# Score products of 64-wide heads issued in pairs, and one weight chunk split inside the double norm

## The chip, the cores and the metric

The kernel runs on one core of a Trainium2 chip. The metric is the device time of one execution in microseconds (us). The core's engines are TensorE (PE, with its weight loads shown as PEld), VectorE (DVE), ScalarE (ACT), GpSimd (POOL) and SyncE (SP), which only issues transfers here. Each runs its own list of instructions in order and waits for the others on semaphores.

## The reference, cut to what matters

Three transformer blocks follow each other on 256 tokens of width 1024. What is computed at the places of the change are attentions whose heads are 64 wide, and the norm between block 1 and block 2:

```python
# block 1, even layer: sliding window, 8 query heads of 64, 2 key/value heads, a sink for each head
logits = jnp.einsum('bkgnqd,bknsd->bkgnqs', qb, kb).astype(jnp.float32) * (DH ** -0.5) + bias
probs = jax.nn.softmax(jnp.concatenate([logits, sink], axis=-1), axis=-1)[..., :-1]
...
# block 2, layer 0 (the "mixer"): differential attention, 8 score heads of 64, beside a short convolution
z = hn @ a_w_in[j]
...
attn = diff_attention(q, k, v, lam, lambda_init, a_subln[j])
...
# block 3: latent attention (8 heads, 96 wide), then sparse attention (8 heads, 64 wide), 256 + 16 keys
s = jnp.einsum('bqhd,bqkhd->bhqk', qb, k_sel, preferred_element_type=jnp.float32) * scale
```

Block 1 ends in `rmsnorm(h, final_gain)` and block 2 begins with `rms_norm(h, ln_mix[0])`, so two norms stand in a row there: the double norm.

## The kernel before

**Weights.** All weight matrices come as one stream of chunks of 1 MB (128 rows, 2048 columns) into a ring of three buffers, in two halves each. ScalarE casts a half to `high` (L252, `split_high`), VectorE subtracts it from the original to get `low` (L261, `split_low`), and SyncE loads the chunk three later into the slot when the subtraction is done (L227). A cast also waits until TensorE has used the chunk three before (`used`). TensorE multiplies with both parts (`times`, L276 to L278: high by high, high by low, low by high). A chunk of an input projection is 48 such products, 24 for each tile of 128 tokens (`chunk_pe`).

**Projections.** Chunk m of a projection goes to PSUM bank m % 2, and ScalarE evicts it (`evac_act`, L1278), scaled by the norm's factor. From the third chunk on TensorE waits for the eviction of the chunk two before (`evac`).

**The double norm.** The first chunk of the mixer is multiplied with h as it is, while the norm's factor is still being worked out; the factor is applied at the eviction, which waits for `scaled`. In `deferred_act` ScalarE squares h, then `roots_act` squares the gained h (L526), when VectorE has made it, and takes two roots (L518). In `scale_twice_dve` VectorE gains h (L579), makes the mean (L562, L564), refines the first root (`newton`, L363 to L371), works out the second mean (L585 to L589), refines the second root, signals `scaled` (L592) and scales h (L595). Behind that, in the programs of the mixer (`mixer_act`, `mixer_dve`), both engines split the third chunk, whose number is `c0 + 2`; the first two were split earlier.

**Attention.** All five attentions are run by `Steps`. Step s on TensorE (`step_pe`) has three parts: the scores of head s (L1051, two products, one for each tile of queries), the product of head s − 2 with the values (L1068), and the transposes of head s − 1 (L1079, in block 3 also L1083). VectorE masks (L1126, signals `masked_l`) and takes maxima (L1130); ScalarE makes the exponentials (L1097, and L1099 where there is a sink; `soft`) and copies the transposed rows (L1111, L1113; `spread`); VectorE scales the output (L1155). Heads take two score banks in turn, so the scores of head s wait for the mask of head s − 2. Other work stands between the steps: in the sliding-window attention and in the sparse attention six products of 512 columns of the output projection (`half_pe`), in the mixer 24 products of a chunk. A 64-wide head lies on rows 0 to 63 of its operands if its number is even, on 64 to 127 if it is odd. The layout of the heads of the latent attention (96 wide) and of block 1's odd layer (128 wide) has no such pairs.

Of the kernel before, what the change touches and what calls it, by code (L numbers as in the profile page):

```python
# [17 lines left out]
NT = SEQ // P  # L18
# [16 lines left out]
TWO = (P, P)  # L35
# [497 lines left out]
def deferred_act(A, k, gain, sem, first, last, twice=False, start=False):  # L533

    turn_act(A, k, TWO, 4, k.xT[0], gain, at=4)
    if start:
        split_high(A, k, k.main, A.chunk)
    A.e.wait_ge(sem, A.passed.get(sem.num, 0) + first)
    A.step(square_act(A, k, 0))
    preload(A, k, ACT.Sqrt)  # L540
    turn_act(A, k, TWO, 4, k.xT[0][:, 4:8, :], gain, at=6, k0=4)
    if start:
        A.e.wait_ge(k.s["x_last"], 16)
    else:
        A.e.wait_ge(*A.next(sem, last))
    A.join()
    A.tell(square_act(A, k, 1), k.s["squared"])
    roots_act(A, k, twice)
    if start:
        split_high(A, k, k.main, A.chunk + 1)  # L550
# [22 lines left out]

def scale_twice_dve(V, k):

# [4 lines left out]
    V.tell(ins, k.s["gained"])  # L580
    var, tmp = mean_dve(V, k)
    newton(V, k, r1, var, tmp)
    V.join()
# [428 lines left out]
class Steps:  # L1012


    def __init__(self, heads, keys, q, kk, values, blocks, scale, bias, out, dv, score, prob, outs, meta=None,
                 sink=None, gate=None):
        self.heads, self.keys, self.q, self.kk, self.values, self.blocks = heads, keys, q, kk, values, blocks
# [26 lines left out]
def step_pe(T, k, a, s):  # L1044

    ident = k.const("ident")
    if s < a.heads:
        if s >= len(a.score):
            T.e.wait_ge(*T.next(k.s["masked_l"]))
        for t in range(NT):  # L1050
            ins = T.e.matmul(a.scores(k, s)[:, a.at[t]:a.at[t] + a.keys[t]], a.q(s, t), a.kk(s)[:, 0:a.keys[t]],  # L1051
                             start=True, stop=True)
        T.tell(ins, k.s["scored"])
    h = s - 2
# [189 lines left out]

def chunk_pe(T, k, m, tiles, after=None, within=None):

# [4 lines left out]
    if m >= 2:  # L1251
        T.e.wait_ge(*T.next(k.s["evac"]))
    for t, rows in enumerate(tiles):
        out = k.ps[0:rows, m % 2, t * CW:(t + 1) * CW] if t < NT else k.ps[0:rows, 2, 0:CW]
        if t == NT and m:
# [12 lines left out]

def evac_act(A, k, dst, m, func=None, at=None, r=None):

    A.e.wait_ge(k.main.used, A.chunk + 1)
    got = k.ps[:, m % 2, :].rearrange("p (t w) -> p t w", t=NT)
    at = m * CW if at is None else at
# [101 lines left out]
class Even:  # L1375
# [31 lines left out]
    def swa(self, k):  # L1407
# [6 lines left out]
        def rows(n):  # L1414
# [6 lines left out]
            (6, 7), ((3, 0), (4, 0)), ((3, 384), (4, 384)), sink=lambda n: sinks[:, head(n):head(n) + 1],  # L1421
            gate=lambda n: pr[:, :, 1536 + head(n) * 64:1536 + (head(n) + 1) * 64])

# [462 lines left out]
def block1_dve(V, k):  # L1886
# [11 lines left out]
    odd_dve(V, k)  # L1898
    scale_twice_dve(V, k)

# [94 lines left out]
class Mixer:  # L1995
# [11 lines left out]
    def steps(self, k):  # L2007
        def rows(h):
# [5 lines left out]
            lambda h: k.const("causal"), lambda h: self.both[:, :, h // 2, h % 2, :], P,  # L2014
            (3, 4), ((5, 0), (6, 0)), ((2, 0), (7, 0)))

# [22 lines left out]
def mixer_pe(T, k):  # L2039
# [3 lines left out]
    for n in range(1, 4):  # L2043
        chunk_pe(T, k, n, TWO)
    jobs = Jobs(T, k, m.jobs, MIXER_BANKS)
# [34 lines left out]
def mixer_act(A, k):  # L2080
# [4 lines left out]
    for n in range(4):  # L2085
        split_high_next(A, k, c0 + n + 2)
        if n == 0:
            scaled(A, k)
        evac_act(A, k, m.pr, n, r=r)
    preload(A, k, ACT.Exp)  # L2090
# [26 lines left out]
def mixer_dve(V, k):  # L2117
# [6 lines left out]
    V.next(k.s["evac"], N_IN2)  # L2124
    for n in range(4):
        split_low_next(V, k, c0 + n + 2)
    V.e.wait_ge(k.s["evac"], evac + 4)
# [986 lines left out]
class Third:  # L3114
# [41 lines left out]
    def dsa(self, k):  # L3156
# [5 lines left out]
        def rows(h):  # L3162
# [4 lines left out]
            lambda h: k.mix[:, :, 512 + h * 64:512 + (h + 1) * 64], 64,  # L3167
            (3, 4), ((5, 0), (6, 0)), ((5, 384), (6, 384)), 7)

# [776 lines left out]
```

## Time and profile before

| | |
|---|---|
| median of 3 runs | 1884.21 us (1884.13 to 1884.23) |
| the profiled execution | 1883.01 us, of which 1880.8 us from the first to the last instruction (the span) |
| TensorE busy | 1827.9 us, 97% of the span |
| VectorE busy | 1402.7 us, 75% |
| ScalarE busy | 1205.2 us, 64% |
| TensorE clock granted, mean | 0.992 of full |

Times in a timeline count from the span's start. A record of TensorE's begins when the product begins; its end is modelled and overlaps the next, so the distance from one start to the next is what a product takes. An fp32 product is two records. Idle time is shown in square brackets with the engine and the line that ended it. In the rows a clock of 1.00 is 2.4 GHz and 0.50 is 1.2 GHz. Block 1's sliding window lies at 95 to 127 us, the double norm at 250 to 261, the mixer's attention at 286 to 327, the sparse attention at 1630 to 1667.

### The profile page before, as it was taken

Reading aid. Unit: us, or ns where it says so; the run is one execution under the profiler, and the core shown is the slowest. Engines: PE = TensorE matmul, PEld = TensorE weight load, DVE = VectorE, ACT = ScalarE, POOL = GpSimd, SP = SyncE. Lnnn points to the kernel's source line nnn. Section 1 sums busy time; section 2 is a strip of 40 time slices with the busy share of each in tenths; the row PEclk is TensorE's granted clock in tenths of the full one; section 3 lists DMA queues with packets and bytes.
Section 4 is the critical chain, followed back from the end, with each engine's and each line's share of the span. In section 5 each row is a group of like instructions: output and inputs, shape, how many; then the busy total and the mean of one; then the engine's idle time right before and its main releaser. Section 6 shows DMA issues by size and latency. Waiting matters only on the chain.

```text
span 1880.8 us, 31987 instructions
## 1 busy us (share of the span) xinstructions
PE 1827.9 (97%) x11013; PEld 1590.8 (85%) x11013; DVE 1402.7 (75%) x2039; ACT 1205.2 (64%) x1897; POOL 71.8 (4%) x109
## 2 busy tenths in 40 slices
PE   8989999999999999999999999999999999999998
PEld 7969889899989878888888888888887888889997
DVE  5575765855566669998989998989999777666555
ACT  6556555544456557877878787878778666454444
POOL 2000000000000020000000000000000033200000
PEclk9999999999999999999999999999999999999999
DMA  8526344465555459999999999999999443136552
GB/s 297 196 92 221 116 135 126 150 201 178 190 168 193 156 162 386 366 374 367 370 363 367 366 373 365 361 361 358 366 362 351 151 136 101 57 107 196 189 189 91
DMA packets 129571, 454.05 MB, mean 241 GB/s; under 512 B 15182, under 2 KB 20206, under 8 KB 129216
## 3 DMA queue, kind: packets, MB, share of 16 engines
q1 hardware_dynamic: 119920, 435.74, 65.6%
q10 hardware_dynamic: 8544, 13.30, 2.2%
q0 software_dynamic: 1008, 3.67, 0.5%
q8 instruction: 65, 1.06, 0.2%
q14 instruction: 34, 0.28, 0.0%
HBM read 450.53 MB, written 5.27 MB: 242 GB/s over the span
## 4 chain that ended last, share of the span: by engine, by line
PE 91%; DVE 5%; ACT 3%; issue 1%; DMA 0%; ACTq 0%; DVEq 0%
PE ps L276 27%; PE ps L277 27%; PE ps L278 27%; PE ps L1068 2%; PE ps L1051 1%; DVE low L261 1%; PE ps L2736 1%; DVE xT_low L342 1%; PE ps L2802 1%; PE ps L410 1%; PE ps L973 1%; PE ps L1079 1%; ACT xT_high L330 1%; ACT high L252 0%; PE ps L2718 0%
## 5 line engine op out<-in xcount | busy, mean ns | idle before, releaser
L261 DVE TENSOR_TENSOR low<-ring,high 128x1024 fp32r<-128x1024 f32 x828 | 980.3, 1223 | 211.9 <-ACT high L252 209.4
L252 ACT CAST high<-ring 128x1024 fp32r<-128x1024 f32 x828 | 834.5, 1050 | 189.1 <-PE ps L278 154.8
L276 PE MATMUL ps<-high,xT_high 128*128 128x256 f32 (+2 forms) x1848 | 639.5, 346 | 20.5 <-DVE xT_low L342 7.1
L277 PE MATMUL ps<-low,xT_high 128*128 128x256 f32 (+2 forms) x1848 | 621.7, 336 | 0.0
L278 PE MATMUL ps<-high,xT_low 128*128 128x256 f32 (+2 forms) x1848 | 619.1, 335 | 0.0
L276 PEld LDWEIGHTS ps<-high,xT_high 128*128 128x128 f32 (+1 forms) x1848 | 347.3, 188 | 63.2 <-issue 14.4
L278 PEld LDWEIGHTS ps<-high,xT_low 128*128 128x128 f32 (+1 forms) x1848 | 347.0, 188 | 40.3
L277 PEld LDWEIGHTS ps<-low,xT_high 128*128 128x128 f32 (+1 forms) x1848 | 348.1, 188 | 33.1
L276 PE MATMUL ps<-high,smallT_high 128*128 128x512 f32 (+2 forms) x582 | 225.0, 387 | 0.7 <-DVE smallT_low L342 0.5
L277 PE MATMUL ps<-low,smallT_high 128*128 128x512 f32 (+2 forms) x582 | 225.3, 387 | 0.0
L278 PE MATMUL ps<-high,smallT_low 128*128 128x512 f32 (+2 forms) x582 | 224.3, 385 | 0.0
L276 PE MATMUL ps<-xT_high,high 128*128 128x256 f32 x704 | 198.4, 282 | 0.6 <-DVE xT_low L342 0.6
L277 PE MATMUL ps<-xT_low,high 128*128 128x256 f32 x704 | 198.6, 282 | 0.0
L278 PE MATMUL ps<-xT_high,low 128*128 128x256 f32 x704 | 197.5, 281 | 0.0
L276 PEld LDWEIGHTS ps<-xT_high,high 128*128 128x128 f32 x704 | 132.2, 188 | 1.8 <-issue 0.9
L278 PEld LDWEIGHTS ps<-xT_high,low 128*128 128x128 f32 x704 | 133.1, 189 | 0.0
L277 PEld LDWEIGHTS ps<-xT_low,high 128*128 128x128 f32 x704 | 132.4, 188 | 0.8
L276 PEld LDWEIGHTS ps<-high,smallT_high 128*128 128x128 f32 (+1 forms) x582 | 109.5, 188 | 24.8 <-DVE smallT_low L342 0.8
L278 PEld LDWEIGHTS ps<-high,smallT_low 128*128 128x128 f32 (+1 forms) x582 | 109.2, 188 | 24.2
L277 PEld LDWEIGHTS ps<-low,smallT_high 128*128 128x128 f32 (+1 forms) x582 | 109.2, 188 | 22.6
L823 ACT ACTIVATE work<-work 128x256 f32<-128x256 f32 x44 | 18.4, 418 | 104.3 <-DVE work L860 104.3
L1278 ACT ACTIVATE proj<-ps,small 128x256 f32<-128x256 f32 x82 | 34.3, 470 | 56.0 <-PE ps L278 56.0
(357 smaller groups left out, 1428.1 us busy)
## 6 DMA issues: line engine op xcount, KB each, us to landing
ring<-in_stream SPq DMA_DIRECT2D x828, 512.0 KB, 5.1
bias_rows<-bias_line ACTq DMA_DIRECT2D x2, 1536.0 KB, 12.8
wide<-in_wide_rows ACTq DMA_DIRECT2D x5, 512.0 KB, 5.4
work<-bias_rows ACTq DMA_DIRECT2D x2, 1024.0 KB, 9.4
h<-in_x SPq DMA_DIRECT2D x2, 512.0 KB, 4.8
work<-bias_rows ACTq DMA_DIRECT2D x2, 512.0 KB, 6.5
token_rows<-mix ACTq DMA_DIRECT2D x1, 1024.0 KB, 4.6
consts<-in_consts ACTq DMA_DIRECT2D x1, 870.0 KB
```

Source lines behind the costliest of these rows:

```text
L252: A.e.copy(k.high[:, slot, cols], k.ring[:, slot, cols]).then_inc(flow.high_made, 1)
L261: V.e.tensor_tensor(k.low[:, slot, cols], k.ring[:, slot, cols], k.high[:, slot, cols].bitcast(F32), ALU.subtract).then_inc(flow.split, 1)
L276: T.e.matmul(out, x[0], w[0], start=start, stop=False, **more)
L277: T.e.matmul(out, x[0], w[1], start=False, stop=False, **more)
L278: return T.e.matmul(out, x[1], w[0], start=False, stop=stop, **more)
L330: ins = A.e.activation(high[:, kt, 0:width], k.ps[:, at + b % 4, n * width:(n + 1) * width], ACT.Copy, scale=g)
L342: ins = V.e.scalar_tensor_tensor(low[:, kt, 0:width], k.ps[:, at + b % 4, n * width:(n + 1) * width], g, high[:, kt, 0:width].bitcast(F32) ...
L410: ins = T.e.transpose(k.ps[:, 4 + b, (n * NT + t) * P:(n * NT + t + 1) * P], k.h[:, t, kt * P:(kt + 1) * P], k.const("ident"))
L973: ins = T.e.transpose(k.ps[0:width, self.banks[n % nb], at:at + P], src, k.const("ident"))
L1051: ins = T.e.matmul(a.scores(k, s)[:, a.at[t]:a.at[t] + a.keys[t]], a.q(s, t), a.kk(s)[:, 0:a.keys[t]], start=True, stop=True)
L1068: ins = T.e.matmul(out, left, a.values(h, b), start=(b == 0), stop=(b == last))
L1278: ins = A.e.activation(dst[:, t, at:at + CW], got[:, t, :], func or ACT.Copy, scale=r[:, t:t + 1])
```

## The change

Three things are done.

1. `Steps` gets a flag `paired`, set for the sliding-window attention, the mixer and the sparse attention. With it an even step issues the scores of heads s and s + 1, tile by tile in turn, and waits for two masks; an odd step issues none.
2. The split of the mixer's third chunk moves into the double norm: ScalarE's two casts behind its last square of h, VectorE's two subtractions behind the first mean. The mixer's own loops then split each chunk one place earlier.
3. The third chunk goes to PSUM bank 2, and TensorE does not wait for an eviction before it.

```diff
@@ deferred_act
     A.tell(square_act(A, k, 1), k.s["squared"])
+    if twice:
+        split_high_next(A, k, A.chunk + 2)
     roots_act(A, k, twice)
@@ scale_twice_dve (block 1 passes V.chunk + 2, block 2 nothing)
     var, tmp = mean_dve(V, k)
+    if ahead is not None:
+        split_low_next(V, k, ahead)
     newton(V, k, r1, var, tmp)
@@ step_pe
-    if s < a.heads:
+    if s < a.heads and not (a.paired and s % 2):
+        group = (s, s + 1) if a.paired else (s,)
         if s >= len(a.score):
-            T.e.wait_ge(*T.next(k.s["masked_l"]))
+            T.e.wait_ge(*T.next(k.s["masked_l"], len(group)))
         for t in range(NT):
-            ins = T.e.matmul(a.scores(k, s)[:, a.at[t]:a.at[t] + a.keys[t]], a.q(s, t), a.kk(s)[:, 0:a.keys[t]],
-                             start=True, stop=True)
-        T.tell(ins, k.s["scored"])
+            for h in group:
+                ins = T.e.matmul(a.scores(k, h)[:, a.at[t]:a.at[t] + a.keys[t]], a.q(h, t), a.kk(h)[:, 0:a.keys[t]],
+                                 start=True, stop=True)
+                if t == NT - 1:
+                    T.tell(ins, k.s["scored"])
@@ chunk_pe
     if m >= 2:
-        T.e.wait_ge(*T.next(k.s["evac"]))
+        evac = T.next(k.s["evac"])
+        if bank is None:
+            T.e.wait_ge(*evac)
@@ mixer_pe
     for n in range(1, 4):
-        chunk_pe(T, k, n, TWO)
+        chunk_pe(T, k, n, TWO, bank=2 if n == 2 else None)
@@ mixer_act
     for n in range(4):
-        split_high_next(A, k, c0 + n + 2)
+        if n < 3:
+            split_high_next(A, k, c0 + n + 3)
         if n == 0:
             scaled(A, k)
-        evac_act(A, k, m.pr, n, r=r)
+        evac_act(A, k, m.pr, n, r=r, bank=2 if n == 2 else None)
@@ mixer_dve
-    for n in range(4):
-        split_low_next(V, k, c0 + n + 2)
+    for n in range(3):
+        split_low_next(V, k, c0 + n + 3)
```

How the order of instructions moves, at three places. Line numbers of the changed kernel are 2 to 11 higher than those of the same lines before (L1058 is the score product, L1076 the product with the values, L1087 the transposes, L1288 the eviction).

ScalarE through the double norm, before (L511 squares h, L526 squares the gained h, L518 is a root, L252 a cast, L1278 the eviction of the first chunk):

```order
L511 ACTIVATE work,small<-h 128x512 [waits act_steps,added]
L511 ACTIVATE work,small<-h 128x512
L526 ACTIVATE mix,small<-work 128x1024 [waits gained]
L526 ACTIVATE mix,small<-work 128x1024
L518 ACTIVATE small<-small 128x2 [waits var_made] x2
L252 CAST high<-ring 128x1024 [waits chunk_used,chunk_landed1_0]
L252 CAST high<-ring 128x1024 [waits chunk_landed1_1]
L1278 ACTIVATE proj<-ps,small 128x256 [waits chunk_used,scaled]
L1278 ACTIVATE proj<-ps,small 128x256
L252 CAST high<-ring 128x1024 [waits chunk_used,chunk_landed2_0]
```

and now:

```order
L511 ACTIVATE work,small<-h 128x512 [waits act_steps,added]
L511 ACTIVATE work,small<-h 128x512
L252 CAST high<-ring 128x1024 [waits chunk_used,chunk_landed1_0]
L252 CAST high<-ring 128x1024 [waits chunk_landed1_1]
L526 ACTIVATE mix,small<-work 128x1024 [waits gained]
L526 ACTIVATE mix,small<-work 128x1024
L518 ACTIVATE small<-small 128x2 [waits var_made] x2
L252 CAST high<-ring 128x1024 [waits chunk_used,chunk_landed2_0]
L252 CAST high<-ring 128x1024 [waits chunk_landed2_1]
L1288 ACTIVATE proj<-ps,small 128x256 [waits chunk_used,scaled]
```

The two casts of slot 1, the third chunk's, stand ahead of the squares of the gained h; behind the roots the casts of slot 2 follow at once.

TensorE in the sliding-window attention, before: from the transposes of step 2 to the product with the values of step 3.

```order
L1079 MATMUL ps<-consts,logit 128x128 [waits soft]
L1079 MATMUL ps<-consts,logit 128x128 x2
L276 MATMUL ps<-high,xT_high 128x512
L277 MATMUL ps<-low,xT_high 128x512
L278 MATMUL ps<-high,xT_low 128x512
L276 MATMUL ps<-high,xT_high 128x512
L277 MATMUL ps<-low,xT_high 128x512
L278 MATMUL ps<-high,xT_low 128x512
L1051 MATMUL ps<-proj 128x128 [waits masked_l]
L1051 MATMUL ps<-proj 128x256
L1068 MATMUL ps<-proj,probT 128x64 [waits spread]
L1068 MATMUL ps<-proj,probT 128x64 x2
```

Now, the scores of step 2 with what stands around them,

```order
L277 MATMUL ps<-low,xT_high 128x512
L278 MATMUL ps<-high,xT_low 128x512
L1058 MATMUL ps<-proj 128x128 [waits masked_l]
L1058 MATMUL ps<-proj 128x128
L1058 MATMUL ps<-proj 128x256 x2
L1076 MATMUL ps<-proj,probT 128x64 [waits spread]
L1076 MATMUL ps<-proj,probT 128x64 x2
```

and from the transposes of step 2 on:

```order
L1087 MATMUL ps<-consts,logit 128x128 [waits soft]
L1087 MATMUL ps<-consts,logit 128x128 x2
L276 MATMUL ps<-high,xT_high 128x512
L277 MATMUL ps<-low,xT_high 128x512
L278 MATMUL ps<-high,xT_low 128x512
L276 MATMUL ps<-high,xT_high 128x512
L277 MATMUL ps<-low,xT_high 128x512
L278 MATMUL ps<-high,xT_low 128x512
L1076 MATMUL ps<-proj,probT 128x64 [waits spread]
L1076 MATMUL ps<-proj,probT 128x64 x2
```

Step 2 has the scores of two heads, and between the products of the output projection and step 3's product with the values none are left.

TensorE where the mixer's third chunk begins, before:

```order
L276 MATMUL ps<-high,xT_high 128x256
L277 MATMUL ps<-low,xT_high 128x256
L278 MATMUL ps<-high,xT_low 128x256
L276 MATMUL ps<-high,xT_high 128x256 [waits evac,chunk_split]
L277 MATMUL ps<-low,xT_high 128x256
L278 MATMUL ps<-high,xT_low 128x256
```

and now:

```order
L276 MATMUL ps<-high,xT_high 128x256
L277 MATMUL ps<-low,xT_high 128x256
L278 MATMUL ps<-high,xT_low 128x256
L276 MATMUL ps<-high,xT_high 128x256 [waits chunk_split]
L277 MATMUL ps<-low,xT_high 128x256
L278 MATMUL ps<-high,xT_low 128x256
```

The wait for an eviction is gone from the first product of the third chunk; the wait for the split stays.

## Rows read from the trace of the kernel before

**Rows 1.** The page's chain that ended last, by engine.

```profile
PE 91%; DVE 5%; ACT 3%; issue 1%; DMA 0%; ACTq 0%; DVEq 0%
```

**Rows 2.** TensorE's timeline, mixer's third chunk: start, length (us), instruction, [idle <-releaser].

```profile
259.59 0.28 PE L278 MATMUL ps<-high,xT_low 128*128 128x256 f32 x1
263.02 0.58 PE L276 MATMUL ps<-high,xT_high 128*128 128x256 f32 x1 [3.15 <-DVE low L261]
```

**Rows 3.** Stretches there: engines' busy us, granted clock, DMA share, GB/s.

```profile
254.30:259.90 5.60, 5.57 (x48) 5.36 (x46) 2.84 (x16) 3.98 (x8) 0.00 (x0) 1.00 0.01 3
259.90:262.90 3.00, 0.00 (x0) 0.00 (x0) 3.00 (x5) 3.00 (x6) 0.00 (x0) 1.00 0.00 0
262.93:266.34 3.41, 3.32 (x15) 3.32 (x16) 3.41 (x5) 2.38 (x4) 0.00 (x0) 0.50 0.92 270
```

**Rows 4.** ScalarE's timeline through the double norm, columns as in rows 2.

```profile
254.08 1.06 ACT L526 ACTIVATE mix<-work 128x1024 f32<-128x1024 f32 x1 [2.04 <-DVE work L579]
...
258.09 1.98 ACT L252 CAST high<-ring 128x1024 fp32r<-128x1024 f32 x2
259.97 0.83 ACT L1278 ACTIVATE proj<-ps,small 128x256 f32<-128x256 f32 x2
```

**Rows 5.** VectorE's timeline through the double norm, columns as in rows 2.

```profile
256.39 0.17 DVE L363 RECIPROCAL small<-small 128x2 f32<-128x2 f32 x1 [2.08 <-ACT small L518]
...
259.29 1.41 DVE L595 TENSOR_SCALAR h<-work,small 128x1024 f32<-128x1024 f32 x2
260.61 6.90 DVE L261 TENSOR_TENSOR low<-ring,high 128x1024 fp32r<-128x1024 f32 x6
```

**Rows 6.** TensorE's timeline, a step of the mixer's attention.

```profile
294.34 0.92 PE L1051 MATMUL ps<-work 64*128 64x128 f32 x4
295.19 0.94 PE L1068 MATMUL ps<-proj,probT 128*128 128x128 f32 x6
```

**Rows 7.** TensorE's timeline, a step of the sparse attention.

```profile
1642.48 0.97 PE L1051 MATMUL ps<-work,proj 64*128 64x144 f32 x4
1643.38 0.43 PE L1068 MATMUL ps<-proj,probM 128*128 128x64 f32 x2
```

**Rows 8.** Stretches of the three attentions, columns as in rows 3.

```profile
102.67:111.99 9.32, 9.32 (x55) 7.04 (x54) 8.52 (x27) 5.29 (x15) 0.00 (x0) 1.00 0.21 63
122.98:126.39 3.41, 1.67 (x14) 1.30 (x13) 2.91 (x14) 1.65 (x6) 0.00 (x0) 1.00 0.01 2
126.39:129.81 3.42, 3.42 (x12) 2.73 (x11) 0.58 (x2) 0.00 (x0) 0.00 (x0) 0.50 0.02 7
287.20:320.00 32.80, 32.80 (x247) 29.53 (x248) 18.85 (x39) 17.91 (x47) 0.00 (x0) 1.00 0.35 114
1639.30:1663.90 24.60, 24.60 (x157) 19.65 (x157) 13.14 (x35) 12.32 (x39) 0.00 (x0) 1.00 0.14 44
```

**Rows 9.** ScalarE's timeline: evictions of the mixer's third and fourth chunk.

```profile
270.47 0.84 ACT L1278 ACTIVATE proj<-ps,small 128x256 f32<-128x256 f32 x2 [5.17 <-PE ps L278]
...
276.13 0.84 ACT L1278 ACTIVATE proj<-ps,small 128x256 f32<-128x256 f32 x2 [2.93 <-PE ps L278]
```

**Rows 10.** TensorE's timeline: index products of heads 0 and 1.

```profile
1558.76 0.98 PE L3202 MATMUL ps<-proj 64*128 64x144 f32 x8
```

**Rows 11.** TensorE's timeline, first transposes of the sparse attention.

```profile
1633.46 0.33 PE L1079 MATMUL ps<-consts,logit 128*128 128x128 f32 x1 [0.56 <-ACT logit L1097]
```

**Rows 12.** TensorE's timeline, waits of the sliding-window attention.

```profile
99.68 0.55 PE L1079 MATMUL ps<-consts,logit 128*128 128x128 f32 x3 [1.06 <-ACT small L1099]
...
124.75 0.55 PE L1079 MATMUL ps<-consts,logit 128*128 128x128 f32 x3 [1.17 <-ACT small L1099]
```

**Rows 13.** VectorE's timeline in the sliding-window attention.

```profile
110.19 0.55 DVE L1126 SCALAR_TENSOR_TENSOR logit<-ps,work 128x384 f32<-128x384 f32 x1
...
113.22 1.23 DVE L261 TENSOR_TENSOR low<-ring,high 128x1024 fp32r<-128x1024 f32 x1 [0.39 <-ACT high L252]
```

**Rows 14.** ScalarE's timeline in the sliding-window attention.

```profile
112.15 1.04 ACT L252 CAST high<-ring 128x1024 fp32r<-128x1024 f32 x1 [2.79 <-PE ps L278]
```

More of the change, by code:

```diff
@@ L571, in scale_h_dve, with scale_twice_dve @@
     return scale_of(k)
-def scale_twice_dve(V, k):
+def scale_twice_dve(V, k, ahead=None):
     gained, r1, r = gained_of(k), first_scale_of(k), scale_of(k)
@@ L1015, in __init__ @@
     def __init__(self, heads, keys, q, kk, values, blocks, scale, bias, out, dv, score, prob, outs, meta=None,
-                 sink=None, gate=None):
+                 sink=None, gate=None, paired=False):
+        self.paired = paired
         self.heads, self.keys, self.q, self.kk, self.values, self.blocks = heads, keys, q, kk, values, blocks
@@ L1239, in load_bias_act, with chunk_pe @@
         A.e.dma_start(bias_of(k)[:, :, t * P:(2 * t + 1) * P], src).then_inc(k.s["bias_loaded"], 16)
-def chunk_pe(T, k, m, tiles, after=None, within=None):
+def chunk_pe(T, k, m, tiles, after=None, within=None, bank=None):
     c = T.chunk
@@ L1251, in chunk_pe @@
     if m >= 2:
-        T.e.wait_ge(*T.next(k.s["evac"]))
+        evac = T.next(k.s["evac"])
+        if bank is None:
+            T.e.wait_ge(*evac)
     for t, rows in enumerate(tiles):
-        out = k.ps[0:rows, m % 2, t * CW:(t + 1) * CW] if t < NT else k.ps[0:rows, 2, 0:CW]
+        out = k.ps[0:rows, m % 2 if bank is None else bank, t * CW:(t + 1) * CW] if t < NT else k.ps[0:rows, 2, 0:CW]
         if t == NT and m:
@@ L1266, in chunk_pe, with evac_act @@
     T.chunk += 1
-def evac_act(A, k, dst, m, func=None, at=None, r=None):
+def evac_act(A, k, dst, m, func=None, at=None, r=None, bank=None):
     A.e.wait_ge(k.main.used, A.chunk + 1)
-    got = k.ps[:, m % 2, :].rearrange("p (t w) -> p t w", t=NT)
+    got = k.ps[:, m % 2 if bank is None else bank, :].rearrange("p (t w) -> p t w", t=NT)
     at = m * CW if at is None else at
@@ L1421, in swa @@
             (6, 7), ((3, 0), (4, 0)), ((3, 384), (4, 384)), sink=lambda n: sinks[:, head(n):head(n) + 1],
-            gate=lambda n: pr[:, :, 1536 + head(n) * 64:1536 + (head(n) + 1) * 64])
+            gate=lambda n: pr[:, :, 1536 + head(n) * 64:1536 + (head(n) + 1) * 64], paired=True)
 EVEN_BANKS, SWA_BANKS = (2, 3), (5, 2)
@@ L1898, in block1_dve @@
     odd_dve(V, k)
-    scale_twice_dve(V, k)
+    scale_twice_dve(V, k, V.chunk + 2)
 def angles_of(k):
@@ L2014, in steps @@
             lambda h: k.const("causal"), lambda h: self.both[:, :, h // 2, h % 2, :], P,
-            (3, 4), ((5, 0), (6, 0)), ((2, 0), (7, 0)))
+            (3, 4), ((5, 0), (6, 0)), ((2, 0), (7, 0)), paired=True)
 MIXER_BANKS = (3, 4, 5, 6)
@@ L3167, in dsa @@
             lambda h: k.mix[:, :, 512 + h * 64:512 + (h + 1) * 64], 64,
-            (3, 4), ((5, 0), (6, 0)), ((5, 384), (6, 384)), 7)
+            (3, 4), ((5, 0), (6, 0)), ((5, 384), (6, 384)), 7, paired=True)
 JOB_BANKS, INDEX_JOB_BANKS, INDEX_BANKS, MLA_BANKS, DSA_BANKS = (3, 4, 5), (0, 6), (6, 7), (3, 4, 5), (3, 4)
```

## The prediction

> **What bounds the kernel now.** I read the chain of waits first: TensorE carries 91% of what ended last [rows 1]. So an edit is worth what it takes off TensorE's own time, or off a wait of TensorE, as long as nothing else is late right behind it. Then I read TensorE's timeline at the two kinds of place that the diff touches.
>
> The first is the start of the second block's mixer. TensorE issues the last product of the second chunk at 259.59 and the first of the third at 263.02, and waited for the `low` half of that chunk [rows 2]. The stretches show what follows: nothing is done from 259.90 to 262.90, and then the granted clock is 0.50 up to 266.34 (1.2 instead of 2.4 GHz) [rows 3]. The third chunk is late because its split stands behind the whole double norm: ScalarE casts it at 258.09, after the second root, and VectorE subtracts at 260.61, after it has scaled h [rows 4, 5].
>
> The second is the score product of a 64-wide head. In the mixer the next operation starts 0.85 us after it (294.34 to 295.19), in the third block's sparse attention 0.90 us (1642.48 to 1643.38) [rows 6, 7]. Whether such time is TensorE's to win depends on the stage. In the mixer VectorE is busy 18.9 of 32.8 us, in the sparse attention 13.1 of 24.6, and TensorE is busy throughout; in the sliding-window attention VectorE is busy 8.5 of 9.3 us, which makes it a second bound there [rows 8].
>
> **The split in the gaps of the norm.** Removed from behind the norm: two casts and two subtractions. They go where both engines are idle. ScalarE stands idle for 2.04 us ahead of the gained h's square at 254.08; two casts take 1.98 us [rows 4]. They fit, and the square that follows is late by 0.05 us at most. Their weights are there: the transfers stand still from 254.30 to 259.90 (DMA share 0.01 [rows 3]), since the ring is full. VectorE is idle for 2.08 us ahead of 256.39, and two of its subtractions take 2.3 (six in 6.90) [rows 5]. Its chain of small operations is thus 0.2 to 0.3 us late, and `scaled` and the scaling of h with it. Nobody on TensorE notices: chunk 3 asks for the eviction of chunk 1. On ScalarE the casts of the fourth chunk now take 258.1 to 260.1, the first eviction 260.1 to 260.9 (it was at 259.97, for it stood behind casts of its own), the casts of the fifth 260.9 to 262.9, the second eviction ends at 263.7. The third chunk, from 259.71, takes 5.66 us (two evictions that wait for TensorE alone start at 270.47 and 276.13 [rows 9]), to 265.4. The slack is 1.7 us. The fourth chunk's `low` half needs VectorE after h, 260.9 to 263.2: slack 2.2 us. The bank 2 that the third chunk takes removes the third wait, that for the eviction of chunk 0, which would else have kept the start at about 260.9.
>
> What this gives: the wait, 263.02 − 259.59 − 0.12 for the product itself = 3.31 us; and the low clock, 263.02 to 266.34 at half rate, 3.32 us for work of 1.66. Together **4.97 us**. What is late next: the ropes wait for the fourth eviction, which moves with TensorE, so the attention starts with the same slack as before. The fewest that I can argue for is 3.3 (the low clock falls somewhere else), the most 5.0.
>
> **The paired products.** The two heads of a pair lie on rows 0 to 63 and 64 to 127 and write to two banks. The trace holds such neighbours already: the index products of two heads, eight records, take 0.98 us, and one head alone, four records of the same shapes, 0.97 [rows 10, 7]. So I take the second head of a pair at nothing, and the saving at the whole place of the odd head. The other end, if the two did not overlap, is a saving near zero. Against pairing speaks a rule of the Trainium skill (TensorE: Matmul & The Clock Gate, "The cost: per-tile semaphore tail"): each increment on a packed product adds some 26 ns, and here each head still signals by itself. By it an estimated 0.3 us of the twelve pairs would be lost; the eight records above carry both heads' signals and show 0.01 us a pair.
>
> The pair needs both masks of the pair before (`masked_l` by 2). The odd one's scores are there a whole step earlier, so VectorE can mask it right after its other work. By stage:
>
> Mixer: four odd heads, 4 × 0.85 = **3.4 us**. Between an even head's scores and its transposes still lie two heads' products with the values, a head's transposes and 24 products of a chunk. TensorE has no wait in these steps now (32.80 of 32.80 us busy [rows 8]), and what goes is 0.85 us between a score and its transposes out of a step of 4.9.
>
> Sparse attention: the first pair wins nothing, since TensorE waits for the first head's exponentials at 1633.46 anyway [rows 11]. The other three give 3 × 0.90 = **2.7 us**; VectorE's 13.1 and ScalarE's 12.3 us of these six steps [rows 8] stay far under the 21.9 that TensorE is left with.
>
> Sliding-window attention: the first pair is lost in the same way (99.68, a wait of 1.06 us [rows 12]). After it VectorE works without a pause: the mask of head 4 at 110.19 comes straight after a subtraction, and names no wait [rows 13]. The one pause until the end is 0.39 us, at 113.22, and it is for a cast that ScalarE began at 112.15, when TensorE had released the chunk [rows 13, 14]. TensorE is there 0.85 us sooner, but VectorE can use 0.39 of it. I take **0.4 us**; the rest comes back as longer waits for the last heads' exponentials, where TensorE already waits 1.17 at 124.75 [rows 12].
>
> **Sum.** 4.97 + 3.4 + 2.7 + 0.4 = 11.5 us. The profiled execution has a span of 1880.8 and a time of 1883.0, the median is 1884.2; the span goes to 1869.3, the median to **1872.7 us**.
>
> **What the clock may add or take.** Between 122.98 and 126.39 TensorE is busy 1.67 us, its longest wait is 1.17, and the clock is at 0.50 from 126.39 to 129.81 [rows 8, 12]. So the clock fell here after small waits. Pairing thins out just this stage, and all later waits shift by 5 to 11 us. A fall of the length seen in both places costs at most 3.4 / 2 = 1.7 us, where TensorE would be full. The Trainium skill (the same page, "Why this matters for your kernels") asks for no idle gap above some 3 us between bursts; the wait at 259.59 agrees, the fall at 126.39 does not. By that rule the shorter waits that pairing leaves would cost nothing; by the row I allow one or two falls more or fewer.
>
> **Rivals.**
> A. A fall of the clock more, or one fewer, at the sliding window or at waits further on: 1874.4 or 1871.0. Both lie inside my range. They are part of the forecast's spread.
> B. The two heads do not overlap in this order of issue (t outer, head inner). Only the norm is left, 1884.2 − 5.0 = 1879.2. For it: no pair of L1051 was ever seen. Against it: rows 10.
> C. The change doesn't do what it says at the norm: the third chunk still stands behind something (a transfer that is late when ScalarE asks for it, which would then also hold the norm's squares behind the cast). Then the pairs alone give 6.5: 1877.7, and with a norm later by the transfer some 1879.
> D. Slower: the thinned attention stages lose the clock. Three stages hold some 25 (102.67 to about 127), 33 and 25 us of steps [rows 8, 12]; a fall costs up to 1.7. From seven falls on the gain of 11.5 is gone; ten would give 1889. In the mixer and the sparse attention TensorE is busy without a break, and pairing adds no wait there, so I hold this for very unlikely.
>
> **How the numbers follow.** Forecast with A: 0.88. B 0.04, C 0.06, D 0.02. The range is 1869.5 (two falls fewer, 3.2 us) to 1877.5 (a fall or two more, or half of the pairs' gain lost), which leaves out B, part of C, and D. A measurement of this kernel can tell about 0.2%, 3.8 us, from no change: faster by more 0.95 (B and C are mostly beyond it too), within 0.03, slower 0.02.
>
> **What would show it.** In the profile after: no TensorE wait for `low` between the second and the third chunk of the mixer, and the clock at 1.00 through it; casts of that chunk between ScalarE's two kinds of squares; eight L1058 records in about 1 us at every second step and none at the others; TensorE's steps in the mixer without a wait; in the sliding-window attention longer waits for the exponentials of heads 6 and 7. I would be wrong if eight such records take 1.5 us or more, if TensorE waits for `masked_l` (a mask on VectorE), or if a wait of over 0.5 us stands before the fourth chunk.

## The result and the profile after

| | before | after |
|---|---|---|
| median | 1884.17 us (1883.29 to 1884.23, 4 runs) | 1873.01 us (1871.18 to 1874.13, 4 runs) |
| ratio | | 0.9937, 95% interval 0.9925 to 0.9948 |
| profiled execution, span | 1883.0, 1880.8 | 1874.04, 1871.9 |

The change makes the kernel 11.2 us faster; 1872.7 was forecast. The profile shows only 9.0 us of it, and why is the larger part of what follows.

What bounds the kernel has not changed. From the page after (busy time and share, then the chain that ended last):

```profile
PE 1818.3 (97%) x11013; PEld 1586.7 (85%) x11013; DVE 1401.5 (75%) x2039; ACT 1204.6 (64%) x1897; POOL 72.0 (4%) x109
...
PE 91%; DVE 5%; ACT 3%; issue 1%; DMA 0%; ACTq 0%; DVEq 0%
```

**The norm.** TensorE's timeline where the second chunk ends and the third begins (start, length, instruction, and an idle time in brackets if there was one), after:

```profile
261.36 0.28 PE L278 MATMUL ps<-high,xT_low 128*128 128x256 f32 x1
261.48 0.28 PE L276 MATMUL ps<-high,xT_high 128*128 128x256 f32 x1
261.59 0.28 PE L277 MATMUL ps<-low,xT_high 128*128 128x256 f32 x1
```

and the stretches around it (busy us of each engine, granted clock, DMA share, GB/s):

```profile
257.70:261.30 3.60, 3.60 (x33) 3.60 (x32) 2.92 (x16) 1.89 (x4) 0.00 (x0) 1.00 0.75 271
261.30:266.80 5.50, 5.50 (x49) 5.50 (x49) 5.44 (x6) 3.63 (x7) 0.00 (x0) 1.00 0.42 128
```

The third chunk starts 0.12 us behind the last product of the second, where 3.43 us lay between them [rows 2], and the clock stays at 1.00 where it was 0.50 [rows 3]. TensorE does not wait before the fourth chunk either. ScalarE's timeline after, which answers to [rows 4]:

```profile
253.32 2.01 ACT L252 CAST high<-ring 128x1024 fp32r<-128x1024 f32 x2
255.49 1.06 ACT L526 ACTIVATE mix<-work 128x1024 f32<-128x1024 f32 x1 [0.15 <-DVE work L581]
...
259.59 1.98 ACT L252 CAST high<-ring 128x1024 fp32r<-128x1024 f32 x2
261.48 0.84 ACT L1288 ACTIVATE proj<-ps,small 128x256 f32<-128x256 f32 x2
```

VectorE's, for [rows 5]:

```profile
255.64 2.35 DVE L261 TENSOR_TENSOR low<-ring,high 128x1024 fp32r<-128x1024 f32 x2
257.91 0.16 DVE L363 RECIPROCAL small<-small 128x2 f32<-128x2 f32 x1
...
260.79 1.41 DVE L599 TENSOR_SCALAR h<-work,small 128x1024 f32<-128x1024 f32 x2
262.11 4.62 DVE L261 TENSOR_TENSOR low<-ring,high 128x1024 fp32r<-128x1024 f32 x4
```

The two casts stand in the gap of 2.04 us between two kinds of squares, the subtractions in that of 2.08. All of this stretch lies 1.4 us later than before, since the sliding-window stage ahead of it took longer (below). Without that shift the reciprocal behind the subtractions (257.91) starts 0.1 us later than before, the scaling of h ends at the same time as before within 0.1, and the first eviction starts at 260.1, where the prediction put it.

**The pairs.** TensorE's timeline in the mixer, for [rows 6]:

```profile
289.65 0.28 PE L278 MATMUL ps<-high,xT_low 128*128 128x256 f32 x1
289.86 0.93 PE L1058 MATMUL ps<-work 64*128 64x128 f32 x8
290.72 0.94 PE L1076 MATMUL ps<-proj,probT 128*128 128x128 f32 x6
291.49 0.49 PE L1087 MATMUL ps<-consts,logit 128*128 128x128 f32 x3
...
294.55 0.28 PE L278 MATMUL ps<-high,xT_low 128*128 128x256 f32 x1
294.67 0.83 PE L1076 MATMUL ps<-proj,probT 128*128 128x128 f32 x6
295.33 0.27 PE L1087 MATMUL ps<-consts,logit 128*128 128x128 f32 x1
```

Eight records of two heads take 0.86 us from the first start to the start of the next operation, where four of one head took 0.85 [rows 6]. The steps without scores show what a score costs besides itself. The operation behind a chunk starts 0.21 us after the last product if it is a score, 0.12 if it is not. The product with the values takes 0.77 us behind a score, 0.66 otherwise. So a score costs 0.85 + 0.09 + 0.11 = 1.05 us. Why it costs the 0.20 around it no run shows. The sparse attention, for [rows 7]:

```profile
1639.47 0.39 PE L278 MATMUL ps<-high,xT_low 128*128 128x512 f32 x1
1639.79 0.97 PE L1058 MATMUL ps<-work,proj 64*128 64x144 f32 x8
1640.69 0.43 PE L1076 MATMUL ps<-proj,probM 128*128 128x64 f32 x2
1640.96 0.39 PE L1076 MATMUL ps<-proj,probT 128*128 128x64 f32 x2
...
1643.57 0.39 PE L278 MATMUL ps<-high,xT_low 128*128 128x512 f32 x1
1643.80 0.33 PE L1076 MATMUL ps<-proj,probM 128*128 128x64 f32 x2
1643.97 0.39 PE L1076 MATMUL ps<-proj,probT 128*128 128x64 f32 x2
```

The same reading gives 0.90 + 0.09 + 0.10 = 1.09 us.

**The sliding window.** TensorE's waits there after, for [rows 12]:

```profile
99.83 0.55 PE L1087 MATMUL ps<-consts,logit 128*128 128x128 f32 x3 [1.91 <-ACT small L1107]
103.06 1.39 PE L1058 MATMUL ps<-proj 64*128 64x128 f32 x8
...
114.62 0.88 PE L1076 MATMUL ps<-proj,probT 128*128 128x64 f32 x6 [1.57 <-ACT probT L1119]
...
122.81 0.55 PE L1087 MATMUL ps<-consts,logit 128*128 128x128 f32 x3 [1.15 <-ACT small L1107]
```

and two stretches, one around its first low clock and one that is its second:

```profile
95.33:104.06 8.73, 6.70 (x37) 4.68 (x37) 6.17 (x17) 5.68 (x18) 0.00 (x0) 0.80 0.33 122
...
124.53:131.36 6.83, 5.24 (x18) 4.06 (x18) 3.21 (x14) 1.65 (x6) 0.00 (x0) 0.50 0.02 5
```

The first wait has grown from 1.06 to 1.91 us, since step 1 has no score of its own any more to put into it. Then the clock is at 0.50 from 100.64 to 104.05 (the mean of 0.80 in the first stretch comes from this; the pair at 103.06 takes 1.39 us) and again for 6.83 us, where before it was low once, for 3.42 [rows 8].

**Where the time went.** All traces hold the same number of TensorE's records, so the same products, found in both, divide the program into stages. In the table a negative number is what a stage takes less than in the profile before, and the last column compares the start of TensorE's last product in the same way. The columns: sliding window and the even layer's rest (95 to 260 us), the mixer's third chunk (260 to 270), the mixer's attention (290 to 328), a chunk at 642 to 655, the stage behind it (655 to 855), the sparse attention (1625 to 1670). The other stages together are within 0.5 us, but for −0.9 in E11. E1 to E11 are the experiments below.

| profile of | window | third chunk | mixer | 642 | 655 to 855 | sparse | end |
|---|---|---|---|---|---|---|---|
| after | +1.28 | −4.91 | −4.11 | −1.57 | +3.23 | −3.05 | −8.94 |
| after, again (E9) | +2.37 | −4.91 | −4.12 | −1.56 | +3.26 | −3.06 | −7.85 |
| norm only (E1) | +1.37 | −4.91 | 0.00 | −1.57 | +3.71 | +0.19 | −1.29 |
| pairs only (E2) | +1.29 | +0.04 | −4.12 | −1.56 | +2.19 | −3.21 | −5.30 |
| no pairs in the window (E3) | −0.33 | −4.91 | −4.12 | −1.57 | +3.29 | −3.07 | −10.76 |
| window's first pair single (E4) | +0.30 | −4.91 | −4.11 | −1.56 | +1.88 | −4.25 | −12.92 |
| the same again (E10) | +0.63 | −4.91 | −4.12 | −1.56 | +2.70 | −4.27 | −11.24 |
| E10, sparse first pair single (E11) | +0.17 | −4.91 | −4.11 | −1.56 | +3.15 | −4.24 | −12.39 |
| split only (E5) | +4.50 | −3.53 | 0.00 | −1.57 | +2.25 | −0.07 | +2.04 |
| bank only (E6) | +0.21 | +0.03 | 0.00 | −0.01 | +3.89 | −1.01 | +3.41 |
| pairs head by head (E7) | −0.08 | −4.91 | −4.10 | −1.57 | +3.42 | −3.04 | −9.94 |
| heads of a pair apart (E8) | −0.64 | −4.91 | −0.14 | −1.57 | −0.02 | −1.14 | −8.26 |

The third chunk and the mixer repeat to 0.02 us. The window does not repeat in two profiles of one kernel (after and E9), and 655 to 855 does not in kernels that are the same there.

### The profile page after: what moved, and what is told of

The parts are those of the page before. It is cut to its first block, busy times and chain, and to the rows that moved or that the text cites. A ratio compares the mean times of both kernels' runs of the same rounds, so it can differ in the third digit from the quotient of the medians.

```text
span 1871.9 us, 31986 instructions
## 1 busy us (share of the span) xinstructions
PE 1818.3 (97%) x11013; PEld 1586.7 (85%) x11013; DVE 1401.5 (75%) x2039; ACT 1204.6 (64%) x1897; POOL 72.0 (4%) x109
## 3 DMA queue, kind: packets, MB, share of 16 engines
q8 instruction: 65, 1.06, 0.2%
## 4 chain that ended last, share of the span: by engine, by line
PE 91%; DVE 5%; ACT 3%; issue 1%; DMA 0%; ACTq 0%; DVEq 0%
PE ps L276 27%; PE ps L277 27%; PE ps L278 27%; PE ps L1076 2%; DVE low L261 1%; PE ps L2747 1%; PE ps L1058 1%; DVE xT_low L342 1%; PE ps L2813 1%; PE ps L410 1%; ACT xT_high L330 1%; PE ps L977 1%; PE ps L1087 1%; ACT high L252 1%; PE ps L2702 0%
## 5 line engine op out<-in xcount | busy, mean ns | idle before, releaser
L261 DVE TENSOR_TENSOR low<-ring,high 128x1024 fp32r<-128x1024 f32 x828 | 979.6, 1222 | 209.1 <-ACT high L252 207.0
L252 ACT CAST high<-ring 128x1024 fp32r<-128x1024 f32 x828 | 833.7, 1049 | 190.3 <-PE ps L278 162.2
L1288 ACT ACTIVATE proj<-ps,small 128x256 f32<-128x256 f32 x82 | 34.4, 471 | 51.1 <-PE ps L278 51.1
```

Source lines behind the costliest of these rows:

```text
L252: A.e.copy(k.high[:, slot, cols], k.ring[:, slot, cols]).then_inc(flow.high_made, 1)
L261: V.e.tensor_tensor(k.low[:, slot, cols], k.ring[:, slot, cols], k.high[:, slot, cols].bitcast(F32), ALU.subtract).then_inc(flow.split, 1)
L1288: ins = A.e.activation(dst[:, t, at:at + CW], got[:, t, :], func or ACT.Copy, scale=r[:, t:t + 1])
```

## The experiments

### E1 and E2: each half alone

E1 takes `paired=True` from all three attentions. E2 keeps it and undoes the edits at the norm.

```diff
# E1, at each of the three
-            ..., paired=True)
+            ...)
# E2
-    if twice:
-        split_high_next(A, k, A.chunk + 2)
...
-    scale_twice_dve(V, k, V.chunk + 2)
+    scale_twice_dve(V, k)
...
-        chunk_pe(T, k, n, TWO, bank=2 if n == 2 else None)
+        chunk_pe(T, k, n, TWO)
...
```

> The changed kernel without any pairing: only the early split and bank 2 of the mixer's third chunk are left. My theory (the norm is worth the 3.3 us wait and 1.6 us of low clock behind it): the third chunk ends 4.9 us earlier against the start than in the kernel before, the sliding window is as before, and the median is 1884.2 - 4.9 = 1879.3, give or take 1.7 for one fall of the clock that moves. Rival (the low clock only moves elsewhere): 3.3 us, 1880.9.

> The kernel before with pairing in all three attentions, split and bank of the third chunk as before. From the trace of the changed kernel: mixer 4.1 us, sparse attention 3.05, and a loss of 1.3 in the sliding window through two falls of the clock: 1884.2 - 4.1 - 3.05 + 1.3 = 1878.4. If the sliding window's loss is not due to pairing but to chance, this gives 1877. Rival (pairs do not overlap, all is the norm): 1884.

E1 measured 1880.43 us (1876.21 to 1881.89, 10 runs) against 1884.09 for before on the same chip, ratio 0.9973 (0.9964 to 0.9983). E2 measured 1877.22 us (1875.55 to 1878.43, 5 runs), ratio 0.9960 (0.9946 to 0.9973). The gains of 3.7 and 6.9 us sum to 10.5, near the change's 11.2. In the table each half has its own stages' gain to 0.2 us and none in the other's, so the halves are independent. E1 has the window as before, and yet takes 1.37 us more there. Its median lies nearer to the rival's 1880.9 than to 1879.3. The profile decides for the third chunk: 4.91 us, and no low clock behind it. That all low clock of an execution has become less by as much, the median does not show.

### E3 and E4: the sliding window without pairs, and with its first pair single

```diff
# E3: in the window's Steps
-            gate=lambda n: ..., paired=True)
+            gate=lambda n: ...)
# E4: in the window's Steps, and in step_pe
+            gate=lambda n: ..., paired=True, singles=2)
...
+    paired = a.paired and s >= a.singles
-    if s < a.heads and not (a.paired and s % 2):
+    if s < a.heads and not (paired and s % 2):
...
```

> The changed kernel with the sliding-window attention alone unpaired. Theory (pairing there makes TensorE wait from 97.6 to 99.8 instead of 98.3 to 99.7, and the clock falls at 100.6; later falls come with it): no fall at 100.6, the clock falls once near 126 as in the kernel before, the chunk that ended 1.8 us later at 133.9 ends where it did before, and the whole is 1.3 to 1.8 us faster than the changed kernel, 1871.5. Rival (the clock's falls have nothing to do with the pairing there, they vary from run to run): the same falls, the same 1873.

> The changed kernel, but in the sliding-window attention heads 0 and 1 are issued singly, one in each step, as before; heads 2 to 7 stay paired. Theory: TensorE has the second head's scores between its waits again, no fall at 100.6, and pairing of the rest gives the 0.4 us that VectorE can use, so the even layer's first output chunk ends 0.4 us sooner than in the kernel before and the whole is at 1871.1. Rival 1 (any pairing there thins out TensorE enough for falls between 112 and 131): as the changed kernel, 1873. Rival 2: TensorE's other pairs give their full 1.0 us each, 1869.

E3 measured 1872.36 us (1871.91 to 1875.68, 5 runs), ratio 0.9941 (0.9927 to 0.9954); E4 1871.18 us (1870.10 to 1874.47, 5 runs), ratio 0.9938 (0.9925 to 0.9952). Both lie within the interval of the change. Pairing in the window is worth nothing that the median shows. The two profiles went the way of the theories: neither has a low clock at 100, and in E3 the clock fell once, at 125.9, and the stage took 0.33 us less than before. E3's median is 0.6 us under the changed kernel's, where 1.3 to 1.8 was expected. In E4 the clock fell twice, at 113.7 and 124.0, so its median at the expected 1871.1 does not speak for the theory.

### E5 and E6: the early split and the bank apart

Both have no pairs. E5 keeps the early split and takes the third chunk back to its old bank and its wait for the eviction of chunk 0. E6 keeps bank 2 without the wait and has the split behind the norm.

```diff
# E5
-        chunk_pe(T, k, n, TWO, bank=2 if n == 2 else None)
+        chunk_pe(T, k, n, TWO)
...
-        evac_act(A, k, m.pr, n, r=r, bank=2 if n == 2 else None)
+        evac_act(A, k, m.pr, n, r=r)
# E6
-    if twice:
-        split_high_next(A, k, A.chunk + 2)
...
-    scale_twice_dve(V, k, V.chunk + 2)
+    scale_twice_dve(V, k)
...
```

> All three attentions single as before; of the edit at the norm only the earlier casts and subtractions stay, and the mixer's third chunk goes to its old bank and waits for the eviction of chunk 0. My theory (the prediction's account of the third wait): the split is there in time, but the eviction of chunk 0, after the casts that follow the second root, holds the start to about 260.9, so TensorE waits some 1.2 us in place of 3.3; the low clock behind the wait goes with it or stays (1.66). The end of the third chunk comes 3.7 us earlier than before if the clock stays high, 2.1 if it falls; 4.9 would say that the bank was needless. Rival (the split alone is the cause, the bank adds nothing): 4.9. Time by the first 1880.5 to 1882, the attentions' clock apart.

> All three attentions single as before; of the edit at the norm only bank 2 and the missing wait for the eviction of chunk 0 stay, the third chunk's split stands behind the double norm as before. My theory: the wait is for the low half (VectorE, after it has scaled h), so TensorE waits the same 3.3 us, the clock falls the same way, and the third chunk ends where it did, within 0.1 us. Rival (the bank matters by itself): 1 us or more earlier. Time 1884, within 1.5 us for the clock elsewhere.

E5 measured 1880.86 us (1879.39 to 1885.05, 10 runs), ratio 0.9980 (0.9970 to 0.9990); E6 1884.69 us (1881.36 to 1886.53, 10 runs), ratio 0.9997 (0.9988 to 1.0007), both against 1884.46. TensorE's timeline at the third chunk of E5:

```profile
264.09 0.28 PE L278 MATMUL ps<-high,xT_low 128*128 128x256 f32 x1
265.51 0.36 PE L276 MATMUL ps<-high,xT_high 128*128 128x256 f32 x1 [1.13 <-ACT proj L1288]
```

and of E6:

```profile
260.09 0.28 PE L278 MATMUL ps<-high,xT_low 128*128 128x256 f32 x1
263.52 0.57 PE L276 MATMUL ps<-high,xT_high 128*128 128x256 f32 x1 [3.14 <-DVE low L261]
```

In E5 the releaser is the eviction (L1288), in E6 the subtraction (L261), as the first theory had it. The split is worth 3.53 us, the bank 1.38 more once the split is early, and nothing by itself. The start in E5, 265.51 less the 4.50 by which the stretch lies late, is 261.0; 260.9 was worked out from the rows. The clock did not fall behind the wait of 1.13 us; behind that of 3.14 in E6 it did (257 to 263 at 1.00, then 3.41 us at 0.50).

### E7 and E8: how the pair must stand in the queue

E7 issues a pair head by head, in place of tile by tile. E8 puts the odd head's scores behind the product with the values and keeps the wait for both masks.

```diff
# E7
-        for t in range(NT):
-            for h in group:
+        for h in group:
+            for t in range(NT):
# E8, in step_pe
+        scores_pe(T, k, a, s)
+    if a.paired and s == 1:
+        scores_pe(T, k, a, 1)
...
         T.tell(ins, k.s["weighed"])
+    if a.paired and s < a.heads and s % 2 == 0 and s:
+        scores_pe(T, k, a, s + 1)
...
```

> The changed kernel, but the four records of a pair's even head are issued before the four of the odd one, in place of alternating. Theory 1 (two products on different rows of the array overlap whatever the order, since the loads of weights and the streams of both heads go side by side): a pair's eight records still take 0.93 to 1.0 us and the mixer gains 4.1 us again. Theory 2 (only neighbours in the queue overlap, so alternating is needed): only the boundary of the two heads overlaps, eight records take 1.5 to 1.7 us, the mixer's gain falls to 0.5 to 1.5 us, the sparse attention's likewise, and the time rises by 5 to 6 us to about 1878.

> The changed kernel, but in every step behind the first pair the odd head's scores are issued behind the even step's product with the values, so that the pair's two heads no longer stand next to each other; the wait for both masks and the early start of the odd head's scores stay. Theory 1 (the gain is the overlap of the two heads on TensorE): the mixer's gain against before falls from 4.1 us to near 1.0 (the first pair alone overlaps; three odd heads cost 0.85 to 1.0 again), the sparse attention's from 3.05 to about 0; time about 1872.9 + 3 + 3 = 1879. Theory 2 (the gain is the earlier scores, which relieve VectorE and the waits): the gains stay within 0.5 us of 4.1 and 3.05 and the time within 1 us of 1873.

E7 measured 1872.45 us (1870.91 to 1873.01, 4 runs), ratio 0.9934 (0.9917 to 0.9951), and 4.10 us in the mixer: neither of the two orders within the pair is better. Its timeline of TensorE:

```profile
288.57 0.93 PE L1058 MATMUL ps<-work 64*128 64x128 f32 x8
289.44 0.82 PE L1076 MATMUL ps<-proj,probT 128*128 128x128 f32 x5
```

The single starts within these eight are 288.575, 288.588, 288.789, 288.801, 288.901, 288.913, 289.119 and 289.132. The records of 128 columns come as the first four and those of 256 as the last four, though each head's 256 columns are issued before the other head's 128. A head has two records of 128 columns, so the second head's first product starts at 288.588, and the first head's 256 columns at 288.901. So the two heads run side by side and not merely one behind the other's load.

E8 measured 1879.24 us (1874.75 to 1883.59, 7 runs), ratio 0.9978 (0.9967 to 0.9990). Its timeline of TensorE in the mixer (L1051 is the score there, L1079 the product with the values, L1092 the transposes):

```profile
288.71 0.92 PE L1051 MATMUL ps<-work 64*128 64x128 f32 x4
289.56 0.94 PE L1079 MATMUL ps<-proj,probT 128*128 128x128 f32 x6
290.43 0.92 PE L1051 MATMUL ps<-work 64*128 64x128 f32 x4
291.28 0.55 PE L1092 MATMUL ps<-consts,logit 128*128 128x128 f32 x3
```

Each head pays its 0.85 us again, and the mixer's gain is 0.14 us. The expectation's 1.0 came from a misreading: a chunk's products stand between the scores of steps 0 and 1, so in E8 not even the first pair is together. Theory 1 holds: the gain is the overlap, not the earlier scores. The sparse attention says the same: its −1.14 is one low clock less, as E6's −1.01, which has no pairs at all. The profiled execution of E8 is the fastest of its seven; the medians are compared.

### E9 to E11: the same kernel again, and single first pairs

E9 is the changed kernel unaltered, E10 is E4 again, E11 has `singles=2` in the sparse attention too.

```diff
# E11, in the sparse attention's Steps
-            (3, 4), ((5, 0), (6, 0)), ((5, 384), (6, 384)), 7, paired=True)
+            (3, 4), ((5, 0), (6, 0)), ((5, 384), (6, 384)), 7, paired=True, singles=2)
```

> The changed kernel once more, unaltered, for a second profile of the same program. My theory (the stages that differ from the sum do so by the clock, and where it falls varies from one execution to the next): the norm gives 4.9, the mixer 4.1 and the sparse attention 3.05 us again, within 0.1, while at least one fall of the clock stands in another place or has another length, and the difference to before at the end of the sliding-window attention (1.4 us later in the first profile) or behind the routing moves by 0.5 us or more. Rival (the loss of 1.4 and the 3.2 us behind the routing belong to the change): both come back within 0.3 us. Time 1871.5 to 1873.5.

> Again the changed kernel with heads 0 and 1 of the sliding-window attention single and the six heads behind them paired, for a comparison on one chip with the changed kernel. Theory 1 (pairing the first two heads starts the first exponential later, and single is better by this): 0.7 to 1.8 us under the changed kernel. Theory 2 (the 1.8 us between the medians before was the clock's spread): within 0.6 us of it.

> As the run before, and the first two heads of the third block's sparse attention single as well. There TensorE waits for the first head's exponentials, 1.42 us in the changed kernel, and the first pair showed no gain (3.05 of the 3 times 1.08 that the odd heads behind it take). Expected: the sparse attention gives 3.05 to 3.3 us, so the time lies within 0.4 us of the run before. Rival (single is worse there, since the odd head's scores fill the wait no longer than before): 2.2 to 2.8 us, time 0.3 to 0.9 us above it.

| | median | ratio to before (1884.59) |
|---|---|---|
| E9 | 1871.96 us (1870.76 to 1875.22, 5 runs) | 0.9932 (0.9919 to 0.9946) |
| E10 | 1871.78 us (1869.96 to 1873.28, 5 runs) | 0.9930 (0.9916 to 0.9944) |
| E11 | 1870.56 us (1870.21 to 1874.00, 5 runs) | 0.9929 (0.9915 to 0.9942) |

E9 shows that the window's loss is not fixed: the same program lost 1.28 us there in one profile and 2.37 in the other. The stage 655 to 855 alone came back alike, 3.23 and 3.26, which the rival asked for. But E6, which has neither the pairs nor the early split, lost 3.89 there, and E8, which has the early split, lost nothing. All rows of the table but E8 lie 1.9 to 3.9 us above the profile of before there, so that profile was a lucky one, and the loss can be put down neither to the pairs nor to the split. Stretches of E9 at its low clocks in the window and in that stage:

```profile
101.53:104.94 3.41, 3.41 (x16) 2.10 (x15) 1.07 (x5) 2.10 (x6) 0.00 (x0) 0.50 0.02 5
125.43:132.26 6.83, 5.37 (x19) 4.30 (x19) 3.34 (x15) 1.65 (x6) 0.00 (x0) 0.50 0.02 5
...
671.56:678.40 6.84, 5.03 (x23) 4.97 (x24) 4.50 (x29) 2.43 (x5) 1.06 (x2) 0.50 0.51 167
692.04:698.80 6.76, 6.76 (x21) 5.70 (x21) 3.75 (x5) 1.32 (x2) 2.26 (x2) 0.50 0.85 304
```

In the first profile the stage's low clock was this:

```profile
667.25:680.90 13.65, 10.97 (x50) 10.84 (x51) 7.03 (x43) 6.42 (x15) 3.17 (x6) 0.50 0.29 96
694.55:697.96 3.41, 3.41 (x10) 2.63 (x9) 1.54 (x2) 0.24 (x1) 2.25 (x2) 0.50 0.94 338
```

Some 17 and 14 us at half clock in two executions of one program.

One thing both profiles of the changed kernel share, though. The clock falls at 100 to 102 us, behind the wait that pairing the first two heads made longer (1.06 to 1.91 us). So it does in three of the four profiles with that pair together (after, E2, E9, not E7), and in one of the nine others (E5, which has no pairs). That points at the first pair as a cause of this fall, as the expectation of E3 had it, and thirteen profiles do not settle it. E10 is 0.2 us from E9, so theory 2 is borne out and the 1.8 us that lay between the medians of after and E4 were spread for the most part; a gain of half a microsecond would not be seen in intervals this wide. E11 is 1.4 us under E9 and 1.2 under E10, where 0.4 at most was expected, with intervals that overlap for the most part, so whether it beats the changed kernel stays open. Its sparse attention gave 4.24 us, over the range named, because the low clock behind 1629 was missing; E4 and E10, with the first pair together, show 4.25 and 4.27 without it. The first pair there makes no difference. These profiles also give the pairs' worth with the clock left out: E6 has no pairs and no low clock there and shows 1.01, so the pairs are worth 4.25 − 1.01 = 3.24 us.

## Why the prediction was right

**The norm, 4.97: held.** 4.91 us in every profile that has both parts. The times on ScalarE were right to 0.1 us; VectorE's chain came 0.1 us late in place of 0.2 to 0.3. The slack was there, and the account of the third wait was tested by E5: 1.38 us for a wait that would have lasted until 260.9. Rival C is out. The low clock went with the wait and did not fall somewhere else nearby.

**Mixer, 3.4: mis-sized, 4.11.** The term was four times the distance from a score to the next start, 0.85. The four starts of [rows 6] do not contain the 0.09 us by which the score itself starts late and the 0.11 by which the product behind it takes longer. They can be seen only beside a step without a score. Four times 1.05 is 4.2.

**Sparse attention, 2.7: mis-sized in the same way, 3.05.** Three times 1.09 is 3.27, and 3.24 is what the profiles without a low clock show. Both profiles compared have a low clock in this stage, before from 1635.1 and after from 1629.8, and the other 0.2 us goes with these. That the first pair gives nothing was right; E11 tested it.

**Rival B, no overlap: out.** The eight records of two heads that the trace of before held [rows 10] were the right row. Its price, 1879.2, is what E8 measured with the heads apart, 1879.24; that it agrees to 0.1 us is luck, for E8's executions lie between 1874.75 and 1883.59. The rule of the Trainium skill (TensorE: Matmul & The Clock Gate, "The cost: per-tile semaphore tail"), by which each signalling product would add some 26 ns, would have meant an estimated 0.3 us. The pairs show 0.86 against 0.85 us from start to start in the mixer and 0.90 against 0.90 in the sparse attention; when a waiting engine sees the signals these records do not show.

**Sliding window, 0.4: not to be seen.** In the profile it was a loss of 1.28. From 95 us up to the chunk that ends at 112 us in before, pairing does gain 0.7 us where the clock has not fallen by then (E4, E7, E10 and E11 alike to 0.01), near the 0.85 of the one odd head whose place has gone by then. Behind it waits come, though not only where they were foretold: 1.57 us at 114.62, where before has none, and 1.02 at 125.97 beside the 1.15 at 122.81. Then the low clocks decide: profiles with all pairs stand at −0.08, +1.28, +1.29 and +2.37, unpaired ones at −0.33, +0.21, +1.37 and +4.50. The fear of rival D, that thinning costs the clock some seven falls or more, did not come true. That it costs none is not shown, as the fall at 100 says; the medians leave room for 1 us or so.

**The clock, rival A.** One or two falls were allowed, worth 1.7 us each. The profile of after differs from that of before by more: one gone at 263 (in the norm's term), one gone at 648, one more at 100, longer ones at 124 and 667, one more at 694. The norm, the mixer and the sparse attention sum to 4.91 + 4.11 + 3.05 = 12.07 us. The differences of the other stages, +1.28 − 1.57 + 3.23, and some 0.15 in the rest take 3.1 of it, which leaves the profile's 9.0. In the medians they nearly cancel: 11.2 us were measured, and 12.6 with E9 (1884.59 less 1871.96). That the forecast is 0.3 us from the median is therefore partly luck. It had 0.4 for the window that is not to be seen, and 1.06 too little for the two others.

What stays open is the low clock at 648.63 of before. E6 has it too; the eleven others of the table show no fall there, whatever half of the change they carry. Yet the same wait stands ahead of it in all thirteen profiles, here in before and in after:

```profile
647.39 0.47 PE L276 MATMUL ps<-high,xT_high 128*128 128x512 f32 x1 [1.81 <-issue]
...
639.77 0.47 PE L276 MATMUL ps<-high,xT_high 128*128 128x512 f32 x1 [1.81 <-issue]
```

So the wait's length does not decide it. That is 1.57 us that may belong to how the program lies in time, or to luck.

## What to carry to other kernels

If an operation has steps with it and steps without it, or can be made to have them, price it by the difference of whole steps: its late start and the first records behind it cost too, here a quarter on top of the place itself. Two fp32 products on 64 rows each, on different halves of the rows, run side by side if they stand together in the queue, in both orders that were tried, and not with another operation between them. Read a gain of a few us stage by stage in more than one profile, for what the clock does in stages with waits differs more between two executions of one program than many an edit is worth.

## What the runs showed of the hardware

- The clock does not depend on the program alone. Two executions of one kernel had half clock for some 17 and 14 us in one stage, and 1.28 and 2.37 us of loss in another.
- At 649 us the clock fell in 2 of 13 profiles, before and E6, in a stage that none of the edits touches and behind a wait of 1.81 us that all 13 have. Behind the wait of 3.1 us at 260 it fell in each of the three that have it (before, E2, E6). After 1.13 (E5) it did not, and in the window, with waits of 1 to 2 us, it fell once to three times. The rule of the Trainium skill that the prediction weighed (TensorE: Matmul & The Clock Gate, "Why this matters for your kernels": no idle gap above some 3 us between bursts) names the one at 260 and none of those in the window.
- The starts of two heads' records lie mostly 6 to 7 ns apart in the changed kernel and 12 to 15 in E7, and TensorE began the second head's first product 0.3 us before the first head's second (E7: 288.588 and 288.901), though it is issued behind that.
